# Six seams of one long kernel: more places for the first weight slabs, sums joined ahead of the matrix engine, and operands made before they are wanted

## The reference, cut to what matters

```python
mod = jnp.einsum('bd,de->be', c_act, w_ada[l]) + b_ada[l]        # c_act = silu(c)
sh1, sc1, g1, sh2, sc2, g2 = jnp.split(mod[:, None, :], 6, axis=-1)
h = rms_norm(x, g_pre_mix[l]) * (1.0 + sc1) + sh1
proj = jnp.einsum('bsd,de->bse', h, w_in[l])
...
y_a = spatial_gating(z_u, z_v, g_sgu_v[l], w_spatial[l], b_spatial[l])
...
y_b = dsa_attention(q, k, v, q_idx, k_idx, p_wi)                 # top-k keys by a score, softmax over them
merged = jnp.concatenate([rms_norm(y_a, g_out_sgu[l]), rms_norm(y_b, g_out_attn[l])], axis=-1)
o = jnp.einsum('bse,ed->bsd', merged, w_out[l])
x = x + g1 * rms_norm(o, g_post_mix[l])
h2 = rms_norm(x, g_pre_ffn[l]) * (1.0 + sc2) + sh2
f = jnp.square(jax.nn.relu(jnp.einsum('bsd,df->bsf', h2, w_ff1[l])))
f = jnp.einsum('bsf,fd->bsd', f, w_ff2[l])
x = x + g2 * rms_norm(f, g_post_ffn[l])
```

## Time and profile before

| | |
|---|---|
| median of 3 executions | 2770.67 us (2770.06 to 2770.99) |
| profiled execution, its own time | 2771.5 us |
| its span, first to last instruction | 2769.8 us |
| PE busy | 2683.5 us, 97% |
| DVE, ACT, POOL busy | 1877.8, 1329.2, 267.7 us |
| mean granted PE clock | 0.994 |

### The profile page before, as it was taken

How to read it: one execution, slowest core, us unless ns; L and a number is a source line. 1 busy time by engine, 2 the same in 40 slices (tenths; PEclk the granted TensorE clock), 3 DMA queues, 4 the chain that set the end, 5 groups by cost and what they waited for, 6 DMA issues and landing times. The chain is left out here.

```text
span 2769.8 us, 41849 instructions
## 1 busy us (share of the span) xinstructions
PE 2683.5 (97%) x16710; PEld 2105.4 (76%) x16710; DVE 1877.8 (68%) x2866; ACT 1329.2 (48%) x1941; POOL 267.7 (10%) x429
## 2 busy tenths in 40 slices
PE   7999999999999999999999999889999999999998
PEld 4856644777888888877778898777878878888886
DVE  7678987568666466684987716667666566646676
ACT  4147766468555434463451114552334655543444
POOL 0115630001000000000000001110000100000000
PEclk9999999999999999999999999999999999999999
DMA  7621100446566888741554433207243656677884
GB/s 273 218 86 32 57 1 1 144 145 232 209 228 228 303 265 300 255 156 38 152 151 130 146 115 110 72 18 234 99 143 128 231 216 231 226 289 257 294 284 149
DMA packets 210898, 474.01 MB, mean 171 GB/s; under 512 B 49584, under 2 KB 70704, under 8 KB 205424
## 3 DMA queue, kind: packets, MB, share of 16 engines
q1 hardware_dynamic: 192784, 393.73, 43.0%
q0 software_dynamic: 17920, 77.61, 7.2%
HBM read 344.09 MB, written 124.29 MB: 169 GB/s over the span
## 5 line engine op out<-in xcount | busy, mean ns | idle before, releaser
L2225 PE MATMUL psum<-merged_operand 128*128 128x512 f32 x1536 | 360.7, 390 | 0.0
L2225 PEld LDWEIGHTS psum<-merged_operand 128*128 128x128 f32 x1536 | 288.4, 188 | 60.7
L2225 PE MATMUL psum<-h_half_operand 128*128 128x512 f32 x1344 | 316.8, 391 | 0.0
L2225 PEld LDWEIGHTS psum<-h_half_operand 128*128 128x128 f32 x1344 | 252.3, 188 | 55.4 <-issue 1.0
L2225 PE MATMUL psum<-h_half_operand,weight_parts_operand 128*128 128x512 f32 x768 | 177.5, 392 | 0.8 <-DVE weight_parts_operand L2732 0.6
L2225 PEld LDWEIGHTS psum<-h_half_operand,weight_parts_operand 128*128 128x128 f32 x768 | 143.6, 188 | 34.1 <-DVE weight_parts_operand L2732 2.7
L3733 PE MATMUL psum<-x_operand,weight_high 128*128 128x512 f32 x448 | 140.6, 395 | 2.1 <-DVE z_mixed L3345 2.1
L3733 PE MATMUL psum<-o_operand,weight_high 128*128 128x512 f32 x448 | 138.4, 390 | 0.0
L3733 PE MATMUL psum<-x_operand,weight_low 128*128 128x512 f32 x448 | 137.9, 389 | 0.0
L2732 DVE TENSOR_TENSOR weight_parts_operand<-weight_ring,weight_parts_operand 128x1024 fp32r<-128x1024 f32 x66 | 80.8, 1224 | 83.6 <-ACT weight_parts_operand L2382 83.3
L2732 DVE TENSOR_TENSOR h_half_operand<-hidden_upper,h_half_operand 128x1024 fp32r<-128x1024 f32 (+1 forms) x58 | 74.1, 1297 | 72.6 <-ACT h_half_operand L2517 51.8
(11 more groups left out here) (658 smaller groups left out, 5927.6 us busy)
## 6 DMA issues: line engine op xcount, KB each, us to landing
o<-in_w_ff SPq DMA_DIRECT2D x80, 512.0 KB, 4.6
merged<-hidden_terms SPq DMA_DIRECT2D x56, 512.0 KB, 6.0
hidden_upper<-in_w_ff_down SPq DMA_DIRECT2D x48, 512.0 KB, 4.8
weight_ring<-in_w_out SPq DMA_DIRECT2D x32, 512.0 KB, 3.4
hidden_terms<-weight_parts POOLq DMA_DIRECT2D x16, 1024.0 KB
hidden_terms<-weight_ring POOLq DMA_DIRECT2D x16, 1024.0 KB, 7.9
hidden_upper<-in_w_ff_up SPq DMA_DIRECT2D x32, 512.0 KB, 4.5
o<-hidden_terms SPq DMA_DIRECT2D x28, 512.0 KB, 5.9
```

Of the source, the lines that this page charges most:

```text
L2225: mm = pe.matmul(bank, w[:, at:at + P], tiles(r, i), start=opens and m == 0, stop=closes and m == 2, skip_group_check=resumed)
```

## The change

It touches six places. In order of time:

- **(a) Opening.** The 16 slabs go to eight places (the four of the ring, two free tiles of a working buffer, two new ones named `slab_places`) and not four; x is loaded in four pieces of 1 MB, with slabs 0 and 1 between the second and the third. DVE scales the first tile of x one slab earlier, the second one between its last two slabs.
- **(b) `select_and_gate`.** `add_bias` of tiles 4 and 5 moves from iteration 30 to 29, that of 6 and 7 from behind the search to iteration 30, and POOL's `gated` of 4 and 5 from behind the last test to iteration 30.
- **(c) First mixing.** Seven DVE additions (`join_first_x`) add the eight squared tiles of x, and PE sums one tile instead of eight, inside product 13. The rounding of weight slabs 15 and 16 moves from DVE to ACT.
- **(d) End of the layer.** Three slabs of the next stage, not two, are split ahead, two of them rounded by ACT; DVE does two tiles of the next norm between the sixth and the seventh `add_second`; the last eight sums of squares are four with fillers before and four without inside the next stage's first loop; products 0 and 1 write to other PSUM banks, so that product 2 does not wait for them to be read.
- **(e) `rwkv_output`.** DVE makes the low parts of all four tiles of the first half before it finishes the last tile of y, and not of two; the load of two gate tiles is issued ahead of 16 small loads.
- **(f) `combine` to the second mixing.** The two share a block, so that no meeting of the engines lies between; ACT rounds the first six input tiles (into `g_b_operand`) and DVE the first weight slab (`next_weight`) during `combine`.

```diff
@@ opening
+    PLACES = 2 * RING
+        spare = K.sbuf(ctx, "slab_places", [P, 2, S])
+        places = [K.ring[:, n, :] for n in range(RING)] + [room[:, 8, :], room[:, 9, :], spare[:, 0, :], spare[:, 1, :]]
-                for half in range(2):
-                    tiles = slice(4 * half, 4 * half + 4)
-                    sp.dma_start(x[:, tiles, :], of[:, tiles, :]).then_inc(landed[half].sem, 16)
-                for s in range(LATER):
-                    if s >= RING:
-                        wait_emptied(sp, s - RING)
-                    sp.dma_start(K.ring[:, s % RING, :], K.dram["w_ada"][s]).then_inc(K.slab_loaded[s % RING].sem, 16)
+                for pair in range(KT // 2):
+                    if pair == 2:
+                        load_slab(0)
+                        load_slab(1)
+                    tiles = slice(2 * pair, 2 * pair + 2)
+                    sp.dma_start(x[:, tiles, :], of[:, tiles, :]).then_inc(landed[pair].sem, 16)
+                for s in range(2, LATER):
+                    load_slab(s)
@@ select_and_gate
-                GATED, ROTATED = {26: (0, 1), 29: (2, 3)}, {12: 0, 13: 1, 14: 2}
+                GATED, ROTATED = {26: (0, 1), 29: (2, 3), 30: (4, 5)}, {12: 0, 13: 1, 14: 2}
-                BIASED = {24: (0,), 25: (1,), 27: (2,), 28: (3,), 30: (4, 5)}
+                BIASED = {24: (0,), 25: (1,), 27: (2,), 28: (3,), 29: (4, 5), 30: (6, 7)}
@@ mix_and_ffn
-                def sum_first_x(many):
-                    for t in many:
-                        wait(pe, sq_made, begin[X2_0] + t + 1)
-                        sum_of(0, tiles(o, t), begins=t == 0, ends=t == KT - 1).then_inc(sq_summed.sem, 1)
+                def sum_first_x():
+                    wait(pe, squares_joined, KT - 1)
+                    sum_of(0, tiles(o, 0)).then_inc(sq_summed.sem, 1)
+                def join_first_x(t):
+                    wait(dve, sq_made, begin[X2_0] + t + 1)
+                    if t > 1:
+                        wait(dve, squares_joined, t - 1)
+                    dve.tensor_tensor(out=tiles(o, 0), in0=tiles(o, 0), in1=tiles(o, t), op=ALU.add).then_inc(squares_joined.sem, 1)
-                    elif first and i in (12, 13):
-                        mix(1, i - KT, lambda: sum_first_x(range(4 * (i - 12), 4 * (i - 11))))
+                    elif first and i == 13:
+                        mix(1, i - KT, sum_first_x, KT - 2)
@@ end of the layer
                     for t in range(KT):
                         square_x(X3_0, 0, t, 3 * KT + t + 1)
+                        if t == 3:
+                            wait(act, later_x_stored, 16)
+                            for early in range(BEGUN):
+                                round_normed(1, early, early)
-                    for t in range(KT):
-                        add_second(0, t, 3 * KT + t)
+                    for t in range(6):
+                        add_second(0, t, 3 * KT + t)
+                    wait_root(7)
+                    normed_tiles(1, range(BEGUN))
+                    for t in range(6, KT):
+                        add_second(0, t, 3 * KT + t)
+                    normed_tiles(1, range(BEGUN, KT))
@@ shift_and_features
+            at = 4 + 2 * n if n < 2 else 2 * (n % 2)
+            return psum[:, at:at + 2, :]
+                            if g == 1 and k == begun:
+                                sum_later_squares(pe)
@@ rwkv_output
-                for k in range(BY_ACT):
+                for k in range(WT):
                     rest_of_y(0, k)
                 last_tile["scale_y"](NT - 1)
                 last_tile["bonus_and_gate"](NT - 1)
                 dve.wait_ge(normed, NT)
-                for k in range(BY_ACT, WT):
-                    rest_of_y(0, k)
@@ combine, build
+                    if n == LAST - 3:
+                        for k in range(4):
+                            round_next(k)
+                    elif n == LAST - 1:
+                        for k in range(4, EARLY_SOURCES):
+                            round_next(k)
+                dve.tensor_copy(next_w, K.ring[:, 0, :]).then_inc(K.slab_high.sem, 1)
-            combine(nc, K, merged, yb, y, g_b, gate_dram[KT:2 * KT].rearrange("t p s -> p t s"), last_four, block)
-            shared.close()
+            begun = combine(nc, K, merged, yb, y, g_b, g_b_operand, gate_dram[KT:2 * KT].rearrange("t p s -> p t s"), last_four, block)
```

More of the change, by code:

```diff
@@ L1783, in mix_and_ffn @@
     if first:
-        takers[begin[Y_0L]] = ("PE", KT + 1)
-        takers[begin[X3_1]:begin[X3_1] + KT] = [("PE", KT + 2 + t) for t in range(KT)]
+        takers[begin[Y_0L]] = ("PE", 2)
+        takers[begin[X3_1]:begin[X3_1] + KT] = [("PE", 3 + t) for t in range(KT)]
     order = []
@@ L1945, in wait_record, with source_high @@
                 wait(eng, record_stored[i % 2], 32 * (i // 2))
+        def source_high(half, k):
+            return tiles(begun[0] if begun and half == 0 and k < EARLY_SOURCES else source[half][0], k)
         def w_high(n):
+            if begun and n == 0:
+                return begun[1]
             return parts_operand[:, (n % 2) * KT * P:(n % 2 + 1) * KT * P]
@@ L2157, in mix @@
                         at = slice(k * P, (k + 1) * P)
-                        high, low = source[half]
+                        high, low = source_high(half, k), tiles(source[half][1], k)
                         for m, (w, h) in enumerate(((w_high(i), high), (w_high(i), low), (w_low(i), high))):
-                            mm = pe.matmul(mix_bank(i), w[:, at], tiles(h, k), start=(k == 0 and m == 0),
+                            mm = pe.matmul(mix_bank(i), w[:, at], h, start=(k == 0 and m == 0),
                                            stop=(k == KT - 1 and m == 2))
-                        if k == KT // 2 and inside:
+                        if k == behind and inside:
                             inside()
@@ L2342, in _ @@
                     sum_squares(5, X3_1)
-                    sum_squares(7, X3_0, idle=2)
+                    sum_last_squares(pe, range(4))
             @block.scalar
@@ L2526, in keep_y @@
                         act.activation(tiles(to, t), psum[:, t, :], ACT.Copy).then_inc(y_kept.sem, 1)
-                for k in range(KT):
+                if not first:
+                    act.wait_ge(K.posted.sem, K.posted.n + 2)
+                for k in range(0 if first else EARLY_SOURCES, KT):
                     round_source(0, k)
@@ L2533, in _ @@
                     if 1 <= i and i + 1 < (15 if first else 16):
+                        round_w(i + 1)
+                    if first and i >= 14:
+                        round_h(2 * (i - 14))
+                        round_h(2 * (i - 14) + 1)
                         round_w(i + 1)
@@ L2776, in rest_of_source @@
                 def rest_of_source(half, k):
[L2777 removed]
                     wait(dve, pair_rounded, half * KT + k + 1)
[L2779 removed]
+                    rest(source_high(half, k), tiles(source[half][1], k), room[:, k, halves[half]]).then_inc(pair_split.sem, 1)
                 def add_to_x(i):
```

213 lines of the change are left out of this document (132 added, 81 removed).

## The result

The changed kernel's median is 2753.62 us (2753.23 to 2754.16, 4 executions) against 2770.83 us for the kernel before (2770.06 to 2773.63, 4 executions): 17.2 us less. The ratio is 0.9936, 95% interval 0.9919 to 0.9953. I had forecast 2760.0 us with a range of 2754.5 to 2766.0.

The account below looks back on a forecast made before the run. PE, busy 2683.5 of 2769.8 us, was taken as the limit. Six terms, 2.8 + 1.0 + 2.2 + 1.9 + 1.6 + 1.1 = 10.6 us, gave a median of 2760.1 us (forecast 2760), range 2754.5 to 2766.

Parts of the forecast that it names:

- (a): Opening: slabs load without the queue held back, slab 9 lands at 29.9 us and scalings end near 42.5; -2.8 us.
- (b): End of the search: earlier gating removes PE's 1.35 us wait before its last sums; -1.0 us.
- (c): First mixing: seven sums fewer on PE, but DVE's chain behind the root keeps part of the gain; -2.2 us.
- (d): End of the layer: four sums lose their fillers and PE's 2.07 us wait for z_mixed goes; -1.9 us.
- (e): `rwkv_output`: low parts made first end PE's 2.69 us wait, so first_two's second part starts earlier; -1.6 us.
- (f): Second mixing: PE starts about 2 us earlier, does three products, waits, then has 45 left; -1.1 us.
- the slow row: Opening: PE's half-speed row of 3.52 us, forecast to stay because the idle gap before slab 9 stays.
- rival of 356 GB/s: Opening: DMAs move 356 GB/s instead of 412, so (a) is worth 0.9 us, time 2762.0; chance 0.08.
- the 6.0 us: First mixing: PE work saved by seven sums less, of which PE was forecast to idle more than half away.
- half-clock stretches that bring a loss: Rival: the time shift brings more half-clock stretches elsewhere, 6.4 us each, three making it slower, 2779.3 us; chance 0.05.
- the one with the whole mixing: Rival: PE has products to do while DVE's chain runs, so the mixing gives all 6.0 us, 2756.3 us; chance 0.15.

Follow-up runs that it names:

- e5: The changed kernel unaltered, run again with a second profile: 2753.03 us, ratio 0.9939 to the kernel before.
- e8: The changed kernel with the first mixing as before (eight sums on PE, slabs 15 and 16 rounded by DVE): 2762.69 us, ratio 0.9972.
- e3: The kernel before with the first mixing's edit alone: 2766.24 us, ratio 0.9983.
- e11: The changed kernel with the end-of-layer edit undone (two slabs split ahead, eight sums with fillers, old PSUM banks): 2759.25 us, ratio 0.9955.
- e1: The kernel before with the new opening alone: 2769.74 us, ratio 1.0002.
- e14: The changed kernel with 12 fillers before PE's first slab, two ahead of each later slab, and the search's old tables: 2757.15 us, ratio 0.9948.
- e9: The kernel before unaltered, with a second profile: 2769.08 us, ratio 0.9992.
- e4: The kernel before with 64 more wait instructions on PE in the opening: 2769.54 us, ratio 1.0001.
- e10: The changed kernel with 96 more wait instructions on PE in the opening: 2758.30 us, ratio 0.9955.

## Why the prediction was wrong

Two steps failed. The sentence "Between the places PE is busy throughout, so a gain at one is carried to the end" put every stage between the six places at nothing; in its place the runs show 2.8 us in the chunk stage and 0.7 us behind the last instruction. And the chain in (c) was sized too long, which made that term 2.2 us for 3.9. Had either of them held, the time would have come inside the range.

- **(a)** held in its mechanism: slab 9 at 29.86 for 29.9, the last scaling at 42.53 for 42.5, 2.82 us for 2.8 in the first profile. That match is in part luck, since both first profiles happened to have the slow row; the means of three give 3.3. The rival of 356 GB/s is refuted by 410 GB/s in each window. The Trainium skill's limit ("DMA: Bandwidth & Descriptors", Specifications) is passed in three windows, with 410 to 414 GB/s; here too the measurement decides. Left out was that the clock of this stretch is a draw: its cost went from nothing (e5, the stage began at 49.6 us) to 6 us (e8, at 55.6) in kernels with this opening. I had argued from the idle time before slab 9 that the slow row stays; it was absent in six of the sixteen profiles without fillers there.
- **(b)** is the step with the wrong sign: -1.0, measured +0.1, with +1.2 in the profile and 0 to -0.5 without the half clock. I had costed the wait as gone and not asked what PE does in its place: it waits once, earlier, and the row behind the wait can run at half clock, which it did in one profile of eight.
- **(c)** is the mis-sized term that the forecast hangs on: "Going through the new order with these durations I come to tile 7 at 599.2". Put on the time axis of the kernel before it was at 594.95 + 2.59 = 597.5 (2.59 us is the shift with which the changed profile entered this stretch), the chain being 18.5 us long and not 19.9. The root came where I put it (576.47 + 2.59 = 579.06 for "about 4 us earlier", 583.29 - 4.2). The two waits for ACT's rounding that I feared are there, 0.86 and 1.08 us before L2777, but in the place of two CASTs and of idle time that the old chain had as well. 3.95 us for 2.2, e3 and e8 agreeing. That PE idles for the rest of the 6.0 us was right: 0.24 + 0.96 + 0.16 us of waits are named in the rows, and the others are starts that came late.
- **(d)** 2.25 for 1.9: from the last sums to the end of `shift_and_features` it took 384.65 us before and 382.4 in every kernel with the edit. The loop's end, which I had held fixed near 1257.1, came earlier too: the third product starts at 1249.82 + 6.53 = 1256.35 on the time axis of the kernel before (6.53 us had been gained by then). The other 0.35 us of the table's 2.6 lie ahead of these sums and are not of this edit, since e3 and e11, which don't have it, show them as well; what brings them is open.
- **(e)** 1.8 for 1.6, **(f)** 1.3 for 1.1: right in mechanism, each a little small. Neither was run by itself. For (e) all profiles agree: from `rwkv_output` to `combine` it took 86.4 to 87.8 us in the seven with the old order and 84.9 to 85.4 in the eleven with the new one. In (f) the three products and the wait behind them are there: PE's fourth product starts some 1.3 us late.
- **The chunk stage** was no term of the sum, and it is the largest miss: 4.8 us in the profile, 2.8 us in the means of three against three (221.7 and 218.9 us). Its products on PE are 64 columns wide, and of the 132 pieces of instructions (16 KB each) that are loaded in the span, 48 are loaded here. Most of the pauses that the profile gives to "issue", that is to nothing it sees, lie in it (others near 305 and 680 us). By the DMA records each of the 37 pauses over 0.5 us in this stage in the eighteen profiles ended 2.1 to 3.1 us after such a piece had begun to load, while a piece comes only every 4.6 us on average; that is a link in time, and no run changes the loading alone. In the means of three, the idle time given to "issue" is 1.9 us in this stage before and 0.5 us in the changed kernel, so that it accounts for 1.4 of the 2.8 us. The clock accounts for some 0.7 us more. The windows of about the last 20 us of the stage, in the first profile of the kernel before and of the changed one:

```profile
1850.00:1870.00 20.00, 13.36 (x311) 10.42 (x301) 12.03 (x29) 9.34 (x17) 1.04 (x1) 0.91 0.01 2
```

```profile
1836.00:1856.00 20.00, 12.78 (x336) 10.08 (x331) 12.86 (x31) 9.25 (x17) 1.04 (x1) 1.00 0.01 3
```

All three profiles of the kernel before have a half-clock stretch there, and PE's last 360 products of the stage take 22.1 to 22.2 us in them. In the changed kernel's three the stretch comes at the very end of the stage or behind it, and they take 21.2, 21.3 and 21.6 us. It does not follow the code: e1, with the old code, has 21.2, and e8 and e14, with the new, have 22.1. So 0.7 us of the 2.8 belong to where that stretch happened to fall. Shown is also that the pauses move and vanish between executions of one kernel (e9) and between kernels that differ in waits alone (e4, e10). That the changed kernel has none in three profiles of three, and its eight variants have one or more each, is not explained. The sum without this stage, 13.1 us, would have put the time at 2757.7, inside the range.
- **Chances.** The 0.05 for half-clock stretches that bring a loss did not come: the stretch near 344 us came, but in the chunk stage the clock went the other way. I gave 0.85 to faster, which came. The rival nearest to the measured time is the one with the whole mixing, 2756.3, and (c) went nearly half of the way to it (3.9 us, between 2.2 and 6.0). The range was too narrow because its spread came from the six places only, and from three executions that lay 0.9 us apart, where 31 later ones spread over 11 us.

## What to carry to other kernels

When PE bounds a kernel, what a removed piece of PE work is worth is the time by which the next chain on another engine starts earlier, less what that chain grows; size it by the old chain's own length before simulating a new order, here 18.2 against 18.5 us. A profile of one execution prices what it shows only to within the half-clock stretches and pauses that happened to be in it: take two or three profiles of the kernel before, and price a stretch by those that agree. And judge an edit worth a microsecond or two by its own stretch of the trace: there (c), (d) and (f) repeated within 0.1 us, while medians of one and the same kernel stood 3.3 us apart.

## What was not expected of the hardware

- Six fp32 sums on PE took 7.08 us in one execution and 5.39 us in another of the same program, by the granted clock (0.57 and 1.00 of it); PE had idled 2.16 us and 0.51 us before them. But a wait of 3.49 us before PE's first slab in e5 was followed by a full clock, and one of 2.43 us by half of it. Over the sixteen profiles without fillers there, idle times of 1.9 to 4.0 us went with a half-clock stretch in the opening in ten, and idle times of 2.6 to 3.5 us with none in six, so idle time alone doesn't foretell it.
- 96 instructions that only pass a semaphore, in idle time of PE, went with 4.7 to 5.3 us more in the median (2758.3 for 2753.6 and 2753.0); where the profile shows a part of it, 1.8 us, it lies 1.6 ms behind them.
- A DVE operation on 128x4 elements took 0.77 us and not 0.16 beside a 128x512 operation of POOL. In all eight profiles in which the two met, it took 0.77 to 0.79 us and ended 0.02 to 0.03 us after POOL's; beside a POOL operation on 128x4 elements the same one took 0.16 to 0.20 us.
